# A per-round vector-matrix product on TensorE turned round: the weight blocks become the stationary operand, the condition vector the one moving column

## What is computed

```
cond = jax.nn.silu(c)
for i in range(DEPTH):                      # DEPTH = 2
    mod = cond @ ada_w[i] + ada_b[i]        # 1024 x 3072
    shift, scale, gate = jnp.split(mod[:, None, :], 3, axis=-1)
    h = rmsnorm(x, norm_w[i]) * (1 + scale) + shift
    y = gdn_mixer(h, ...) if i % N_MIXERS == 0 else fox_mixer(h, ...)
    x = x + gate * y
```

## Time and profile before

| | |
|---|---|
| time, median of 3 runs | 1774.71 us (1774.26 to 1775.61) |
| time of the profiled execution | 1774.77 us |
| its span in the profile | 1773.0 us |
| TensorE busy | 1684.9 us, 95% of the span |
| VectorE busy | 1167.7 us, 66% |
| ScalarE busy | 923.5 us, 52% |
| the eight rounds | about 231 to 462 us of the span |

### The profile page before, as it was taken

How to read it: one execution, slowest core, us unless ns; L and a number is a source line. 1 busy time by engine, 2 the same in 40 slices (tenths; PEclk the granted TensorE clock), 3 DMA queues, 4 the chain that set the end, 5 groups by cost and what they waited for, 6 DMA issues and landing times.

```text
span 1773.0 us, 34401 instructions
## 1 busy us (share of the span) xinstructions
PE 1684.9 (95%) x11772; PEld 1556.0 (88%) x11772; DVE 1167.7 (66%) x2364; ACT 923.5 (52%) x1711; POOL 353.0 (20%) x223
## 2 busy tenths in 40 slices
PE   6899989999999997999999999989999999999998
PEld 5899778888899886999899999989999988888887
DVE  2686377777544656547745999978888765555554
ACT  1665523232344555555444444458988855455444
POOL 2000000000000000400002787766656500000000
PEclk9999999999999999999999999999999999999999
DMA  9656310101644442442563565554444455555553
GB/s 271 193 185 189 118 48 25 48 24 48 222 135 143 119 131 81 156 127 96 167 147 93 164 176 167 166 153 139 143 131 138 143 189 193 196 190 192 195 193 130
DMA packets 211808, 255.54 MB, mean 144 GB/s; under 512 B 15911, under 2 KB 193803, under 8 KB 211723
## 3 DMA queue, kind: packets, MB, share of 16 engines
q1 hardware_dynamic: 211723, 254.39, 46.9%
HBM read 253.29 MB, written 1.05 MB: 143 GB/s over the span
## 4 chain that ended last, share of the span: by engine, by line
PE 75%; DVE 10%; DMA 5%; issue 4%; ACT 3%; SPq 2%; DVEq 0%; POOL 0%; ACTq 0%; POOLq 0%
PE ps L1955 21%; PE ps L2468 20%; PE ps L2450 9%; DMA raw<-in_u_experts 4%; PE ps L2438 3%; PE ps L1975 2%; PE ps L2105 2%; PE ps L2094 2%; DVE raw L1730 2%; PE ps L2106 2%; PE ps L2185 2%; SPq L538 2%; PE ps L2084 2%; PE ps L2026 1%; PE ps L2252 1%
## 5 line engine op out<-in xcount | busy, mean ns | idle before, releaser
L652 POOL TENSOR_TENSOR w_lo<-raw,w_hi 128x1024 fp32r<-128x1024 f32 x128 | 307.8, 2408 | 343.3 <-ACT w_hi L1088 343.3
L1955 PE MATMUL ps<-x_hi,w_hi 128*128 128x256 f32 x1088 | 314.2, 289 | 10.4 <-DVE x_lo L1220 5.3
L1955 PE MATMUL ps<-x_lo,w_hi 128*128 128x256 f32 x1088 | 309.8, 285 | 0.0
L1955 PE MATMUL ps<-x_hi,w_lo 128*128 128x256 f32 x1088 | 309.6, 285 | 0.0
L1916 DVE TENSOR_TENSOR w_lo<-raw,w_hi 128x1024 fp32r<-128x1024 f32 x124 | 152.0, 1226 | 143.3 <-ACT w_hi L1188 143.3
L1955 PEld LDWEIGHTS ps<-x_hi,w_hi 128*128 128x128 f32 x1088 | 210.9, 194 | 14.0 <-issue 7.7
L1188 ACT ACTIVATE w_hi<-raw 128x1024 fp32r<-128x1024 f32 x124 | 131.6, 1061 | 168.0 <-PE ps L2468 168.0
L1955 PEld LDWEIGHTS ps<-x_lo,w_hi 128*128 128x128 f32 x1088 | 210.9, 194 | 0.3 <-issue 0.2
L1955 PEld LDWEIGHTS ps<-x_hi,w_lo 128*128 128x128 f32 x1088 | 210.7, 194 | 0.0
L1088 ACT ACTIVATE w_hi<-raw 128x1024 fp32r<-128x1024 f32 x128 | 134.8, 1053 | 121.3 <-DVE raw L1730 121.3
L2413 PE MATMUL ps<-x_hi,w_hi 128*128 128x256 f32 x576 | 166.8, 290 | 10.4 <-ACT arena L1110 10.2
(11 more groups left out here) (383 smaller groups left out, 3926.4 us busy)
## 6 DMA issues: line engine op xcount, KB each, us to landing
raw<-in_u_experts SPq DMA_DIRECT2D x512, 128.0 KB, 2.7
raw<-in_v_experts SPq DMA_DIRECT2D x128, 512.0 KB, 3.2
arena<-in_ada_w SPq DMA_DIRECT2D x20, 1024.0 KB, 5.2
raw<-in_a_w_in SPq DMA_DIRECT2D x12, 1024.0 KB, 5.4
arena<-in_a_w_in SPq DMA_DIRECT2D x12, 1024.0 KB, 5.3
raw<-in_b_w_in SPq DMA_DIRECT2D x8, 1024.0 KB, 5.6
arena<-in_b_w_in SPq DMA_DIRECT2D x8, 1024.0 KB, 5.7
raw<-in_w_in SPq DMA_DIRECT2D x8, 1024.0 KB, 5.4
```

The lines of the kernel that those rows point to most:

```text
L652: pool.tensor_tensor(UTL[e], UT[e % 2], UTH[e].bitcast(F32), ALU.subtract).then_inc(utl_ready, 1)
L1955: ins = mm(o[:, b * S:b * S + S], w[:, slot, kk, b * P:b * P + P], xx[:, (kk + turn) % KC, :], start=(kk == 0 and n == 0), stop=(kk == k - ...
```

## The change

TensorE's `modulator` now takes the weights as the stationary operand, in blocks of 128 x 128 (8 row blocks for each of 2 column blocks), and moves the one column condT[:, kk] past each. The products come out as columns at once: bank 6 holds two columns of 128 numbers. VectorE's part shrinks to the copy of these two columns. The count on `mod_diag` in the rounds goes, and the wait before `modulation(1, ...)` is on `ada_free` in its place. What SyncE loads, and at which signals, is as before.

```diff
             def modulator(r):
                 v.wait_ge(raw_free, r.count(1, 8 + N_ADA + 1))
-                v.tensor_tensor(DIAG, two(ps[6][:, 0:TW]), bcast(ident, 2), ALU.mult).then_inc(ada_free, 1)
-                v.wait_ge(ada_free, r.count(1, 11))
-                v.tensor_reduce(MC2, DIAG, AX_X, ALU.add).then_inc(mod_diag, 1)
-                v.wait_ge(mod_diag, r.count(2, 9))
-                v.tensor_scalar(MC[:, bass.ds(r.count(2), 2)], MC2, 1.0, None, ALU.mult).then_inc(mod_diag, 1)
+                v.tensor_scalar(MC[:, bass.ds(r.count(2), 2)], ps[6][:, 0:2], 1.0, None, ALU.mult).then_inc(ada_free, 1)
...
-            v.wait_ge(mod_diag, 8 + 2 * GQ)
+            v.wait_ge(ada_free, 10 + GQ)
             modulation(1, MC[:, 0:8], MC[:, 8:16], 4)
...
                 pe.wait_ge(ada_free, r.count(1, 10))
-                for kk in range(KC):
-                    ins = mm(ps[6][:, 0:TW], CONDR[:, kk, :], RAW[2][:, kk, :], start=(kk == 0), stop=(kk == KC - 1))
+                for cc in range(2):
+                    for kk in range(KC):
+                        ins = mm(ps[6][:, cc:cc + 1], RAW[2][:, kk, cc * 128:cc * 128 + 128], condT[:, kk:kk + 1],
+                                 start=(kk == 0), stop=(kk == KC - 1))
                 ins.then_inc(raw_free, 1)
```

## The result

In the runs on record with the prediction the changed kernel took 1775.93 us (median of 12) against 1772.67 us before (12 runs): ratio 1.0019, interval [1.0010, 1.0028]. A second set on one chip gave 1776.20 us (11 runs) against 1771.49 us (25 runs), ratio 1.0023 [1.0015, 1.0032]. So the change makes the kernel slower, by 0.2%, some 3 to 5 us. Forecast were 9 us, with 3.4 as the least in the forecast's own range (1778 to 1791 us). The measured time lies inside the wider range of 1770 to 1790 us only because that one was drawn down to take in rival A.

A forecast was written before the change was run, and what follows sets the result against it. TensorE, busy 95% of the span, was taken as the bound, with VectorE counting only where TensorE waits. Seams -4.3, blocks +0.7 and clock falls +12.6 gave +9.0 on 1774.7, so 1783.7 us, range 1770 to 1790.

The forecast's parts named there:

- the forecast's own range: Clock-falls case: five to fourteen slow stretches behind the modulator blocks, net +3.4 to +16.0 us, 1778 to 1791 us.
- rival A: TensorE's clock stays up, as loads or neighbouring level products count as work: 1771.1 us, chance 0.27.
- part 1: Seams between rounds: VectorE's three instructions become one copy, TensorE waits less for the mask, 4.3 us gained over seven seams.
- part 2: TensorE's modulator block at full clock: 32 instructions at 0.111 us, 3.55 us for 3.46, +0.7 us over eight blocks.
- part 4: TensorE's clock falls behind seven of eight modulator blocks, nine slow stretches at 1.4 us each, +12.6 us.
- nine slow stretches: Clock term: falls behind seven of eight blocks, two lasting twice as long, costing 9 x 1.4 = 12.6 us.
- C: Rival: the clock falls, but slow stretches overlap TensorE's next wait and hide; about 1776 us, chance 0.05.
- B: Rival: the clock stays and the block's loads go at the lower bound of 0.07 us each; 1760.6 us, chance 0.03.
- D: Rival: the seam gains nothing, as freed time moves to another wait; 1775.4 us with steady clock, chance 0.05.

The follow-up runs named there:

- cols128: Changed kernel with 128 equal moving columns past each weight load in place of one, VectorE copying columns 0 and 128: 1767.77 us, ratio 0.9978 against before.
- split1: Changed kernel (one moving column) with its block in three parts, the later two between and after level 5's products: 1769.05 us, ratio 0.9983 against before.
- split128: cols128 with its block in three parts, the later two between and after level 5's products: 1763.53 us, ratio 0.9957 against before.
- row_short: Kernel before with its TensorE block kept, VectorE's part cut to one two-element copy, the row-to-column turn left out: 1766.90 us, ratio 0.9970.

## Why the prediction was right in its parts and wrong in its size

**Bound and seam (part 1): right.** The seam closed to the 0.45 us named for it. Its worth was put at 4.3 us and is 5.3 us in the rounds, 4.6 us in the medians. Most of what the sum left out is the 0.1 us that TensorE loses after each of the seven stalls. The support from the earlier trace rows was weaker than it seemed: one of the eight waits, of 1.1 us, is no seam, so that 3.4 us are left for the seams. It is still there in the changed kernel:

```profile
PE ps L2103 <- DVE arena L1407: 1.1, 1, 1.1
```

**Block (part 2): right.** 3.51 us for 3.55. The estimate of 3.4 us that went by the Trainium skill ("TensorE: Matmul & The Clock Gate", "LDWEIGHTS (loading the stationary operand)") holds to 0.1 us.

**Clock (part 4): the fall was right, its price was mis-sized.** In both profiles of the changed kernel the clock falls behind every block, eleven slow stretches where nine were put, three of the falls long. (The Trainium skill's rule of a monitor for how busy the array is, same page, section "Part 1: The HAM clock gate (the "warmup" mystery)", agrees with the falls. These runs add that weight loads alone did not keep the clock up.) The price of one was taken as 1.4 us, from 16 against 27 matmuls in the earlier trace rows. It is 0.96 us. So the clock costs 10.6 us in the rounds where 12.6 was forecast, and the seam gives 5.3 where 4.3 was. The net in the rounds is +5.9 us. The two errors of the clock's term ran against each other, which is luck: at nine stretches the price was 4.0 us too high (9 x 0.44), and the count was short by two, 1.9 us (2 x 0.96).

Why 1.4 was too much: the fall comes right behind the block, and there, in the kernel before, TensorE waits anyway. Between 281.81, where level 5 starts in cols128, and the next round's first product at 286.08, it starts 24 instructions in 4.27 us, 2.7 us' worth at 0.111. In the changed kernel the same 24, from 284.88 to 290.15, take 5.27 us: 1.0 us more, with 3.4 us of it at half the clock. The row of the transposes there, first in cols128 and then in the changed kernel, shows where the rest went:

```profile
284.48 0.75 PE L2070 MATMUL ps<-small,arena 128*128 128x128 f32 x4 [0.38 <-DVE arena L1394]
```

```profile
288.54 0.74 PE L2070 MATMUL ps<-small,arena 128*128 128x128 f32 x4
```

Apart from the seam's own, TensorE's longest waits are those of the transposes after level 5 for VectorE's L1394. In the waits from 240 to 460 us, before and then cols128:

```profile
PE ps L2074 <- DVE arena L1394: 2.7, 7, 0.4
```

```profile
PEld ps L2070 <- issue: 3.8, 7, 0.5
...
PE ps L2070 <- DVE arena L1394: 2.7, 7, 0.4
```

and the changed kernel, which has no row for TensorE's wait on L1394 in this window:

```profile
PEld ps L2070 <- issue: 0.5, 2, 0.3
```

At half the clock TensorE gets there late, VectorE is done, and the wait has gone into the slow matmuls. Where split1 has filled these waits, nothing absorbs the slow clock, and a slow stretch costs the 1.4 us of the forecast. The two pairs of kernels show it. That split1 has only long falls does not explain it: compared fall by fall, a round with a long one (two stretches) takes 30.38 us from block to block in the changed kernel against 28.37 in cols128, 2.0 more, and 30.25 in split1 against 27.40 in split128, 2.85 more. The executions of split1 give a price like that of its profile: its two slowest (1777.57 and 1777.37 us, clock 0.980) and its two fastest (1762.07 and 1762.58, clock 0.989 and 0.990) lie 15.1 us apart, for 34 us of slow time or ten stretches, an estimated 1.5 us each.

**From +5.9 us in the rounds to +3.3 and +4.7 in the medians.** Over all executions the mean clock tells how many slow stretches there were. In the first set it was 0.9909 for before (25 runs) and 0.9805 for the changed kernel (11 runs). Slow time is (1 - clock) x 2 x span, since the clock is either 1.00 or 0.50; that makes 32 and 69 us; the difference is 37 us, or 10.9 stretches of 3.4 us. That agrees with the profile's eleven: over many runs the falls elsewhere are as many as before. With the seam's 4.6 us the medians put a stretch at (4.7 + 4.6) / 10.9 = 0.85 us. What is left between 5.9 and the medians is not traced to a cause, and is within the spread: outside the rounds each execution has its own falls (between the rounds and the experts' loop the ten profiles have two to nine slow stretches, two in that of after and five in that of before), and the stage from the rounds' end to the experts' loop (TensorE's L2413 in before) took from 500.8 to 512.2 us in the ten profiles. In the profile of after it was 500.8 and in that of before 505.2, so that the two spans came out equal. What sets these falls was not tried.

**The failing step, in one line:** "nine slow stretches cost 9 x 1.4 = 12.6 us" took the price from one stretch elsewhere, 1.4 us, and applied it to a place where TensorE waits; measured there it is 0.96 us. With 0.96 for a stretch, 5.3 for the seams and 0.4 for the blocks the same sum gives +3.7 us for nine stretches, and +5.7 for the eleven that there were, against 5.9 in the rounds. (The 0.96 comes from these rounds themselves, so this tests only the rest of the sum. That +3.7 is near the +3.3 of the medians is chance.)

Of the rivals, C came nearest: its 1776 us is what was measured, though no sum led to that number. It said that slow stretches overlap TensorE's next wait, and was put aside with "this can hide no more than a few tenths each". They hid 0.4 of 1.4 us each, which over eleven stretches is 4.8 us. That is more than the whole gap in the rounds (9.0 against 5.9 us); the two stretches that the forecast had too few filled in the rest. A (the clock stays, 1771.1 us) is what cols128 does, -3.7 us against the -3.6 worked out for it. B is refuted by the block's 3.51 us, D by row_short.

## What to carry to other kernels

A float32 matmul with one moving column cost as much TensorE time here as one with 128 (0.11 us), and behind a run of 32 of them TensorE's clock fell. Move as many columns as cost nothing (here 64 or 128 equal ones, and the clock stayed), and put such matmuls where the engine waits. To mix those of one column with full ones helped only in part: in split1's profile there are three falls in place of eight, but each costs more, since no wait is left to hide it.

The price of a slow stretch is the stream it covers less the waits in it. Take it at the place where it falls.

To turn a row into a column on TensorE by making the data the stationary operand is worth it when the engine that did the turning stood between two products. Here that alone was 4.6 us (row_short) of the 8.6 by which split128 beats the kernel before.

## What the runs showed of the hardware

- Weight loads alone do not hold TensorE's clock at 2.4 GHz: in the changed kernel's stretch from 281.4 to 284.8 us, with 32 loads and no gap, the clock was 1.00, and 0.51 in the next. With 128 or 64 columns past each of the same loads no such fall came in the rounds of their profiles; with 32 there were four, behind half of the blocks.
- A float32 matmul's start-to-start time is 0.11 us for 1, 32, 64 and 128 moving columns (blocks of 32 in 3.49 to 3.57 us). So the moving columns do not set it up to 128. The weight load of 128 columns is the same in all four; its size was not varied, so that it sets the 0.11 us is argued and not shown.
- Accumulating one and the same PSUM column in successive matmuls 0.11 us apart costs nothing visible (the changed kernel's block, 32 instructions in 3.51 us).
- After a stall TensorE loses a further 0.1 us: from the first L2105 to the first L2106 it is 0.32 us in before, and 0.22 for the same two (L2101 and L2102) in row_short, where it has not stood.
